# Half the modulation first: four rows of the first norm ahead of the other four in a float32 two-block transformer kernel

## What is computed

```python
mod = c @ w_ada[l] + b_ada[l]
shift, scale, gate = jnp.split(mod, 3, axis=-1)
h = _rmsnorm(x, norm_g[l]) * (1.0 + scale[:, None, :]) + shift[:, None, :]
proj = h @ w_in[l]
(q_a, k_a, v_a, z_a, q_b, k_b, v_b, z_b,
 f_logit, g_logit) = jnp.split(proj, split_points, axis=-1)
y_a = _from_heads(_stick_breaking(_to_heads(q_a, N_HEADS_SB), _to_heads(k_a, N_HEADS_SB),
                                  _to_heads(v_a, N_HEADS_SB)))
```

## Time and profile before

| What | us |
|---|---|
| Median of three runs | 1335.87 (1335.82 to 1336.31) |
| The profiled execution's own time | 1332.21 |
| Its span | 1330.4 |
| PE busy in the span | 1290.0 (97%) |
| Start of the first matmul of a projection | 40.29 |

### The profile page before, as it was taken

One profiled execution on the slowest core, in us unless ns is written; L12 is line 12 of the kernel. 1 busy time (PEld: TensorE's weight loads), 2 busy tenths in 40 slices (PEclk: granted clock), 3 DMA queues, 4 the chain that ended last, 5 costly groups with the idle time before them and its releaser, 6 DMA issues.

```text
span 1330.4 us, 17281 instructions
## 1 busy us (share of the span) xinstructions
PE 1290.0 (97%) x6354; PEld 1072.9 (81%) x6354; DVE 751.4 (56%) x1292; ACT 568.5 (43%) x919; POOL 735.8 (55%) x858
## 2 busy tenths in 40 slices
PE   5999999999999999999999999999999999999997
PEld 5778888878888878887777997888888888888885
DVE  5757776334334348499787535765546715651554
ACT  2555565445555336322445664344434313332331
POOL 0642543433333566577343797543649967885782
PEclk9999999999999999999999999999999999999998
DMA  9621223222423642223223353321323332333321
GB/s 329 230 81 40 84 76 141 89 95 72 126 88 119 229 144 90 89 86 96 79 64 112 112 178 111 108 64 41 102 64 95 111 111 95 95 96 98 93 94 63
DMA packets 41699, 142.80 MB, mean 107 GB/s; under 512 B 4624, under 2 KB 5008, under 8 KB 40464
## 3 DMA queue, kind: packets, MB, share of 16 engines
q1 hardware_dynamic: 41616, 141.71, 33.0%
HBM read 131.21 MB, written 8.39 MB: 105 GB/s over the span
## 4 chain that ended last, share of the span: by engine, by line
PE 78%; DVE 14%; ACT 3%; issue 2%; DMA 2%; POOL 1%; DVEq 0%; SPq 0%; ACTq 0%; POOLq 0%
PE ps L135 77%; DVE tm L148 3%; DVE ac L148 3%; DVE tm L145 2%; ACT tm L142 2%; DMA raw<-units 2%; PE ps L139 1%; DVE x L148 1%; DVE ma L148 1%; DVE zh L156 1%; ACT wh L142 1%; POOL wl L145 0%; POOL ycl L145 0%; DVE cb L145 0%; DVE rtl L145 0%
## 5 line engine op out<-in xcount | busy, mean ns | idle before, releaser
L145 POOL TENSOR_TENSOR wl<-raw,wh 128x256 fp32r<-128x256 f32 x804 | 681.3, 879 | 541.3 <-ACT wh L142 540.9
L142 ACT ACTIVATE wh<-raw 128x1024 fp32r<-128x1024 f32 x201 | 212.1, 1056 | 320.1 <-PE ps L135 309.6
L135 PE MATMUL ps<-hh,wh 128*128 128x512 f32 x872 | 345.2, 396 | 0.0
L135 PE MATMUL ps<-hl,wh 128*128 128x512 f32 x872 | 341.2, 391 | 0.0
L135 PE MATMUL ps<-hh,wl 128*128 128x512 f32 x872 | 341.0, 391 | 0.0
L135 PEld LDWEIGHTS ps<-hh,wl 128*128 128x128 f32 x872 | 164.5, 189 | 34.9
L135 PEld LDWEIGHTS ps<-hh,wh 128*128 128x128 f32 x872 | 164.6, 189 | 34.5 <-DVE tm L145 0.4
L135 PEld LDWEIGHTS ps<-hl,wh 128*128 128x128 f32 x872 | 164.8, 189 | 33.0
L148 DVE SCALAR_TENSOR_TENSOR tm<-cb,par_sb,tm 128x512 f32<-128x512 f32 x88 | 87.1, 989 | 50.5 <-ACT tm L142 47.2
L145 DVE TENSOR_TENSOR tm<-tm,tm 128x512 f32<-128x512 f32 (+3 forms) x106 | 88.2, 837 | 40.2 <-ACT tm L142 37.3
L142 ACT ACTIVATE tm<-tm 128x512 f32<-128x512 f32 (+3 forms) x109 | 54.4, 531 | 93.6 <-DVE tm L148 77.5
(11 more groups left out here) (309 smaller groups left out, 2359.0 us busy)
## 6 DMA issues: line engine op xcount, KB each, us to landing
raw<-units SPq DMA_DIRECT2D x217, 512.0 KB, 3.5
kept<-ge SPq DMA_DIRECT2D x16, 256.0 KB, 2.3
tm<-kept SPq DMA_DIRECT2D x16, 256.0 KB, 3.6
tm<-gate_w SPq DMA_DIRECT2D x12, 256.0 KB, 4.1
x<-xin SPq DMA_DIRECT2D x2, 1024.0 KB, 9.5
x<-xin SPq DMA_DIRECT2D x1, 2048.0 KB, 9.9
out<-x SPq DMA_DIRECT2D x8, 256.0 KB, 2.1
kv<-kvt SPq DMA_DIRECT2D x1, 1536.0 KB, 7.5
```

The source lines that it names most:

```text
L135: return self.none if self.e is None else self.e.matmul(out, lhs, rhs, start=start, stop=stop, skip_group_check=skip)
L142: return self.none if self.e is None else self.e.activation(out, in_, func, **kw)
L145: return self.none if self.e is None else self.e.tensor_tensor(out, a, b, op)
```

## The change

The modulation is split by features instead of by scale and shift. `("ada", a, k)` is now, for k's 128 rows of `w_ada`, 512 columns of scale and 512 of shift, of features 512 a to 512 a + 511. So after eight of these units gain and shift of rows 0 to 3 are known, and after sixteen those of rows 4 to 7.

- **Loads.** The sixteen units no longer go through the ring: each has a place of its own, `ADA[j]`, over memory that is used later (`HH`, `HL`, two slots each of `WH` and `WL`, and others). SP issues them, the first four projection units and three other loads without any wait.
- **DVE.** Eight steps of half 0 (the root's inverse ahead of the last), `mod_pair(0)`, rows 0 to 3 and their low parts with two steps of half 1 between them, six more steps, `mod_pair(1)`, then rows 4 to 7.
- **PE.** `ada_sums` for half 0 behind `spread`. After values' units 0 and 1 (rows 0 to 3) come q's first half, `mod_end` for half 1, and k's first half; then values' units 2 and 3, and the second halves of q and k.
- **Ring.** The units' order is av 0, av 1, aq 0, ak 0, av 2, av 3, aq 1, a gate, az 0, ak 1, az 1, a gate. Since PE uses them in the order av 0, av 1, av 2, av 3, aq 0, ak 0, az 0, the refills stand in this second order on ACT and POOL (`FIRST`), and SP issues in the first.

```diff
 def unit_order():
-    u = [("ada", part, k) for part in (1, 0) for k in range(8)]
-    u += [("av", i) for i in range(4)]
-    u += [("aq", 0), ("ak", 0), ("az", 0)]
-    for c, br in ((1, "a"), (2, "a"), (3, "a"), (0, "b")):
+    u = [("ada", a, k) for a in range(2) for k in range(8)]
+    u += [("av", 0), ("av", 1), ("aq", 0), ("ak", 0), ("av", 2), ("av", 3)]
+    first = beside("a", 1, 0)
+    u += first[0:2] + [("az", 0)] + first[2:5]
+    for c, br in ((2, "a"), (3, "a"), (0, "b")):
         u += beside(br, c, c - 1 if c else 3)
...
+FIRST = [("av", 0), ("av", 1), ("av", 2), ("av", 3), ("aq", 0), ("ak", 0), ("az", 0)]
...
-        mod_end(1, 0, MA)
         bank[7] = (s_sqrt, ("x",))
         spread("x", 7)
         bank[7] = (s_ht, ("1", 7))
-        ada_sums(0, 1, MA2)
+        ada_sums(0, 0, MA)
+
+        def second_half(u):
+            if u == 2:
+                qkz("a", 0, "q", 0)
+                mod_end(1, 6, MA2)
+                qkz("a", 0, "k", 0)
...
-        vproj("a", "av", "1")
-        qkz("a", 0, "q", 0)
+        vproj("a", "av", "1", second_half)
+        take(6)
...
         qkz("a", 0, "q", 1)
-        qkz("a", 0, "k", 0)
         qkz("a", 0, "k", 1)
...
-        hi(UNITS[N_ADA])
-        hi(UNITS[N_ADA + 1])
-        act.wait_ge(s_modc, 0)
+        hi(("av", 0))
+        hi(("av", 1))
         for k in range(KC):
-            if k in (2, 4):
-                hi(UNITS[N_ADA + 1 + k // 2])
+            act.wait_ge(s_modc, k // 4)
             act.wait_ge(s_ht, "1", k)
             act.fn(HH[:, k, :], TM[(3 + k) % 7][:, :], ACT.Identity, bias=sm[:, k:k + 1]).then_inc(*s_hh.up("1", k))
+            if k == 3:
+                hi(("aq", 0))
+                hi(("ak", 0))
+                refill(("av", 0))
+                refill(("av", 1))
...
+        for k in range(KC):
+            if k == 7:
+                dve.wait_ge(l_con, 0)
+                root_inverse("x")
+            mod_step(0, k, MA)
+        mod_pair(0, 0)
+        dve.wait_ge(s_gain, "g", 0)
+        dve.wait_ge(s_spread, "x")
+        row(0)
+        row(1)
+        low_row(0)
+        row(2)
+        low_row(1)
+        mod_step(1, 0, MA2)
+        low_row(2)
+        row(3)
+        mod_step(1, 1, MA2)
+        low_row(3)
+        for k in range(2, KC):
+            mod_step(1, k, MA2)
+        mod_pair(1, 6)
...
         for j in range(N_ADA, N_ADA + RING):
             low(UNITS[j])
-        for name in UNITS[N_ADA:PLACE["az", 0] + 1]:
+        for name in FIRST:
             refill(name)
...
-            if j >= RING:
...
+            if j >= N_ADA + RING:
+                sp.wait_ge(s_wh, UNITS[j - RING])
+                sp.wait_ge(s_wl, UNITS[j - RING])
             sp.dma(RAW[s][:, :], units[j]).then_inc(*l_raw[s].up(j))
...
+        for j in range(N_ADA):
+            sp.dma(ADA[j][:, :], units[j]).then_inc(*l_ada[j].up("ada"))
...
+            if j in (5, 7, 13, 15):
+                raw(N_ADA + (5, 7, 13, 15).index(j))
+        sp.dma(CONT[:, :], con[:, 0:CO + 8]).then_inc(*l_cont.up(0))
+        sp.dma(MKR[:, :], msk).then_inc(*l_msk.up(0))
+        sp.dma(MEMT[:, :, :], memin).then_inc(*l_mem.up(0))
```

More of the change, by code:

```diff
@@ L329, in build @@
     MA2 = at("ma2", [P, U], F32, a1 + 4096)
+    o_ada = [h0, h0 + 4096, h0 + 16384, h0 + 20480] + [w0 + 16384 * x + 4096 * y for x in (1, 2) for y in (2, 3)]
+    o_ada += [h0 + 8192, h0 + 12288, h0 + 24576, h0 + 28672] + [a1 + 8192 + 4096 * x for x in range(3)] + [vb0 + 20480]
+    ADA = [at(f"ada{j}", [P, U], F32, o) for j, o in enumerate(o_ada)]
     off[0] = a1
@@ L1803, in add_square, with mod_step, mod_pair @@
                 parts_of((gen, f), t0 if f == 6 else t, f - 6)
-        def mod_step(part, k, ma):
-            j = PLACE["ada", part, k]
-            dve.wait_ge(l_raw[j % RING], j)
+        def mod_step(a, k, ma):
+            j = 8 * a + k
+            dve.wait_ge(l_ada[j], "ada")
             dve.wait_ge(l_par, 0)
             if k == 0:
-                dve.ts(ma[:, :], RAW[j % RING][:, :], pcol("c", k), ALU.mult).then_inc(*s_mod.up(part, k))
+                dve.ts(ma[:, :], ADA[j][:, :], pcol("c", k), ALU.mult).then_inc(*s_mod.up(a, k))
             else:
-                w = slice(512 if k == 7 and part == 0 else 0, U)
-                dve.wait_ge(s_mod, part, k - 1)
-                dve.stt(ma[:, w], RAW[j % RING][:, w], pcol("c", k), ma[:, w], ALU.mult, ALU.add).then_inc(*s_mod.up(part, k))
+                w = slice(512 if k == 7 and a == 0 else 0, U)
+                dve.wait_ge(s_mod, a, k - 1)
+                dve.stt(ma[:, w], ADA[j][:, w], pcol("c", k), ma[:, w], ALU.mult, ALU.add).then_inc(*s_mod.up(a, k))
+        def mod_pair(a, b):
+            g, o = sm[:, 8 + 4 * a:12 + 4 * a], 4 * a
+            dve.wait_ge(s_modp, a)
+            dve.tt(g, PS[b][:, 0:4], prow("b_ada", 4, 8 + o), ALU.add).then_inc(*s_gain.up("sum", a))
+            dve.tt(sm[:, o:o + 4], PS[b][:, 4:8], prow("b_ada", 4, o), ALU.add).then_inc(*s_modc.up(a))
+            dve.wait_ge(s_gain, "sum", a)
+            dve.ts(g, g, 1.0, ALU.add).then_inc(*s_gain.up("one", a))
+            dve.wait_ge(s_gain, "one", a)
+            dve.tt(g, g, prow("norm_g", 4, o), ALU.mult).then_inc(*s_gain.up("g", a))
         def mod_out(part, b):
@@ L1826, in row, with low_row @@
                     ALU.mult).then_inc(*s_ht.up("1", k))
[L1828 to L1847, removed]
+        def low_row(k):
+            dve.wait_ge(s_modc, k // 4)
             dve.wait_ge(s_hh, "1", k)
@@ L1851, in vector_program @@
                     ALU.subtract).then_inc(*s_hl.up("1", k))
+        for k in range(KC):
[19 more added lines that the diff above has]
+        mod_pair(1, 6)
+        dve.wait_ge(s_gain, "g", 1)
+        row(4)
+        row(5)
+        for k in range(4, KC):
+            low_row(k)
             if k < 6:
@@ L2451, in pool_program @@
             low(UNITS[j])
-        for name in UNITS[N_ADA:PLACE["az", 0] + 1]:
+        for name in FIRST:
             refill(name)
         pool.zero(f32(FT[:, :])).then_inc(*s_fz.up(0))
-        for name in UNITS[PLACE["az", 0] + 1:PLACE["oa", 0]]:
+        for name in UNITS[N_ADA:PLACE["oa", 0]]:
+            if name in FIRST:
+                continue
             refill(name)
@@ L2560, in sync_program @@
         b0 = PLACE["bq", 1] + 2 * RING
-        for j in range(RING, len(UNITS)):
+        for j in range(N_ADA + RING, len(UNITS)):
             done = UNITS[j - 2 * RING] if j >= 2 * RING else None
```

60 lines of the change are left out of this document (27 added, 33 removed).

## The result

| | before | changed |
|---|---|---|
| device time, median (20 runs each, in turn on one chip) | 1334.82 us (1330.56 to 1337.62) | 1337.12 us (1334.82 to 1340.77) |
| ratio to before, 95% interval | | 1.0024 (1.0015 to 1.0032) |
| profiled execution: time, span | 1332.21, 1330.4 | 1339.95, 1338.2 |

The changed kernel is slower by 0.24%, 3.2 us by the ratio (2.0 to 4.3). The prediction had 1339.0 against 1335.87, a ratio of 1.0023.

A forecast was written before the change was run, and what follows sets the result against it. PE is busy for 97% of the span, so only stretches where it waits or does other work, here the start, can move. Terms -3.9 + 1.7 + 0.3 + 1.35 + 2.9 + 0.8 = +3.15 on 1335.87 gave 1339.0, range 1334.0 to 1344.0.

The forecast's parts named there:

- 1. Start: Start of the kernel: the first projection comes at 36.4 instead of 40.29, minus 3.9.
- 2. The sums in the stream: The other half's modulation sums, 16 one-column records on PE inside the projection stream at full clock: plus 1.7.
- 3. The wait in front of them: PE waits before the second half's sums for six DVE steps of 1.69 each, alternating with POOL: plus 0.3.
- proportional bound: Upper bound for the wait before the second half's sums: DVE steps slow in proportion beside POOL to 2.18, wait 3.1.
- 4. Rows 4 to 7: Behind the second half's sums, PE waits 0.35 + 1.0 for low parts of these rows: plus 1.35.
- a sign against 2. and 4.: A granted clock under 1 between 53 and 65 would show the sums and rows 4 to 7 terms wrong.
- 5. The late load: Behind z's end (Z), place 28's load lands at Z + 4.0, delaying ACT's copy and head 0's chain: plus 2.9.
- 6. The clock behind it: After head 0's wait the clock falls a little earlier, and head 1's scores run wholly at 1.2 GHz: plus 0.8.
- No wait: Rival at place 28's load: down by Z + 0.5, so the late load is no wait; 1335.3, chance 0.15.
- shorter wait: Rival at place 28's load: it lands with its neighbour, and the clock costs nothing extra; 1336.9, chance 0.12.
- Clock up through head 0: Rival at 96 to 104: the clock stays up, 3.4 back, with no late load; 1331.9, chance 0.10.
- Proportional slowing: Rival at the second half's sums: DVE slows in proportion and the clock falls; +9.45, 1345.3, chance 0.13.

The follow-up runs named there:

- the second traces: Both kernels profiled once more without any edit, for a second trace each: changed 1336.48, before 1334.41, one run each.
- the pieces of 512: From the changed kernel, POOL's low parts of the first six places taken in two instructions of 512 columns instead of four of 256: 1343.07, one run.
- the fillers: From the changed kernel, ten matmuls of 512 columns whose result nobody reads added in head 0: 1336.22 us, ratio to before 1.0004.

## Why the prediction was right, point by point

- **1. Start**, -3.9: it was -4.2, as worked out, to 0.3 (36.07 for 36.4). What the working did not know is that the start of before differs by 1.9 between two traces, since it hangs on the loads; the changed kernel's start differs by 0.9 over five traces, with the start of its squares. The profiled execution of before was the earlier of the two, so the change may gain more here on average than its first trace says: 6.1 between the second traces. The risk that sixteen loads hold up X did not come in a size that matters: squares start at 10.92 to 11.80 in those five, and at 11.20 and 11.46 in before.
- **2. The sums in the stream**, +1.7: 1.81.
- **3. The wait in front of them**, +0.3: 0.18. Steps of 1.61 for the 1.69 put down, by the turns that were assumed and that the pieces of 512 showed. The proportional bound (a wait of 3.1) is refuted.
- **4. Rows 4 to 7**, +1.35: the idle times are 0.24 + 0.21 + 0.87 = 1.32, but by the distances of the matmuls the rows cost 2.0 (3.38 - 1.36), as each interruption takes more than its idle time. The term is too small by 0.7. From the first projection to z the changed kernel needs 3.2 more than before in its second trace, for a forecast of 3.35, and this closeness is luck: some 4.3 for the sums and the rows by the same count, less some 1.3 at the beginning, mostly because the clock rose 2.1 sooner behind the first projection (5.2 before, 3.1 and 3.0 in the changed kernel's traces), which no term held. In its first trace it is 4.9, with a fall of the clock at 60 that the sum left out and that the prediction had named as a sign against 2. and 4.; "next to two short waits" was the right place to doubt it. It came in one trace of two, and in neither of the kernels with the load first or the fillers (windows from 60 to 63 at 1.00 and 0.95).
- **5. The late load**, +2.9: the copy at Z + 4.0 as forecast (86.22 - 82.25 = 3.97; 84.56 - 80.67 = 3.89 in the second trace), and issuing the load first gave 2.9 back at the last sum of head 0. The prediction's Z - 0.75 for the tenth low part does not follow from its own terms (-5.45 + 1.6 + 2.9 = -0.95); the trace has 81.40, Z - 0.85, and nothing hangs on it. This is the term that decides the sign of the result, and the diff shows no wait for it: it stands in the order of SyncE's queue.
- **6. The clock behind it**, +0.8: too small. With 5. it was to be 3.7 from Silu to Silu, and it was 3.8 and 4.4; with the load first, where nothing waits longer than before, 1.5 were still there. So this term measures about 1.5, by one trace. It was put down as a consequence of the late load, and a good part of it was not: the clock was down for about 10 in the kernel without the late load, over 13 with it, 7 in before. Which difference ahead of head 0 makes it 10, one trace does not tell.
- **The sum**: +3.15, measured 3.2 (2.0 to 4.3). Much of that closeness is luck: terms 4 and 6 were too small by 0.7 each, the sooner rise of the clock was left out, and the gain at the start is larger against one of the two traces of before. Up to the second Silu the first traces give +4.5 and the second ones +1.6, so the traces confirm the mechanism and not the sum to a tenth. The time of 1339.0 is 1.9 above the measured median: 1.05 is the base, 1335.87 from three runs for 1334.82 from twenty, and 0.85 that the medians differ by 2.3 where the ratio over the runs gives 3.2.
- **The rivals.** No wait, shorter wait: refuted by the copy's 3.37. Clock up through head 0: not in the changed kernel; with fillers it is to be had, and brought 1 to 3 in one kernel and nothing in the other instead of 3.4; a wait and a fall come later there. Proportional slowing: refuted.

## What to carry to other kernels

Before splitting work so that the first piece is ready early, look for what can start earlier without a split. Here dropping a ring's waits alone moved the start by 1.7 and handing over one result in two pieces by 1.2 more, with no wait in exchange up to z, while the split of the features bought 4.2 at the head of a stream that is 97% busy and paid 3.2 of them back before z. When the order of use is changed, walk the queue that issues the loads as well: a load stands behind every wait of the ones in front of it, and here moving one load in that order gave back 2.9 and made a slower kernel one that can't be told from before. And where two engines take turns, a shorter instruction on the side that is not urgent shortens the turns of the other.

## What the runs showed of the hardware that was not expected

- DVE's steps of 1024 columns took 1.61 beside POOL's instructions of 256 columns and 2.07 beside those of 512, for 1.28 alone: what a DVE instruction loses beside POOL depends on the length of POOL's instruction, not on its share of time.
- With three matmuls that nobody reads, in 0.87 of TensorE's waiting, the granted clock stayed at 1.00 where it was at 0.5 for about 7 without them, and the kernel was not faster for it.
- In the traced execution of the kernel with ten fillers the granted clock is 0.95 wherever the other traces have 1.00 (0.941 on average, where the other eleven runs of this kernel have 0.989 to 0.990), while its matmuls of 512 columns stand at the same distance:

```profile
89.25 0.39 PE L135 MATMUL ps<-hh,wl 128*128 128x512 f32 x1
89.48 0.39 PE L135 MATMUL ps<-hh,wh 128*128 128x512 f32 x1
```

0.23, as in every other trace at 2.4 GHz. It belongs to the execution and not to the fillers; what it stands for is open.
